# First attention: the division by the softmax sums moves from the probabilities to the outputs

## The reference, cut to what matters

```python
def dsa_mixer(x, cos, sin, w_in, w_o):       # bsz 1, L 512
    proj = x @ w_in                          # q: 16 heads x 64, k, v: 4 heads x 64, index q, k, weights
    ...
    score = jnp.einsum('bqh,bqhs->bqs', iw_b, jax.nn.relu(s))
    score = jnp.where(causal[None], score, -jnp.inf)
    _, sel = lax.top_k(score, top_k)         # top_k = 128 of up to 512 keys
    ...
    logits = jnp.einsum('bqgrd,bqkgd->bqgrk', q_b, k_sel) * A_HEAD_DIM ** -0.5
    logits = jnp.where(valid[:, :, None, None, :], logits, -jnp.inf)
    p = jax.nn.softmax(logits, axis=-1)
    o = jnp.einsum('bqgrk,bqkgd->bqgrd', p.astype(v.dtype), v_sel)
    ...
    return out @ w_o
```

## Time and profile before

| | us |
|---|---|
| median of 3 runs (1941.14 to 1942.45) | 1941.49 |
| the profiled execution | 1947.47 |
| its span | 1945.5 |
| PE busy | 1869.9 |
| DVE (VectorE) busy | 1184.5 |
| ACT (ScalarE) busy | 734.1 |
| POOL (GpSimd) busy | 136.5 |
| scores of the first unit start, in the span | 123.91 |
| output projection starts, in the span | 202.40 |

### The profile page before, as it was taken

How to read it: one execution, slowest core, us unless ns; L and a number is a source line. 1 busy time by engine, 2 the same in 40 slices (tenths; PEclk the granted TensorE clock), 3 DMA queues, 4 the chain that set the end, 5 groups by cost and what they waited for, 6 DMA issues and landing times.

```text
span 1945.5 us, 23033 instructions
## 1 busy us (share of the span) xinstructions
PE 1869.9 (96%) x9172; PEld 1507.9 (78%) x9172; DVE 1184.5 (61%) x2191; ACT 734.1 (38%) x1146; POOL 136.5 (7%) x136
## 2 busy tenths in 40 slices
PE   9989999999999999999999999789899899999997
PEld 7765788878888888788888888677556698888885
DVE  4989676555556676577544546766775554333437
ACT  4447343232223434544222223535554352222221
POOL 0343000000000151000000000000230000000000
PEclk9989999999999999999999999989999899999998
DMA  6210425434442212234343342031001413323221
GB/s 203 66 65 2 152 84 167 161 130 138 144 149 70 74 57 66 66 108 134 127 130 108 118 142 88 23 109 44 1 1 60 146 33 99 108 87 108 87 87 44
DMA packets 116874, 184.04 MB, mean 95 GB/s; under 512 B 7152, under 2 KB 71792, under 8 KB 113696
## 3 DMA queue, kind: packets, MB, share of 16 engines
q1 hardware_dynamic: 115376, 177.77, 27.7%
q0 software_dynamic: 1392, 4.82, 0.9%
HBM read 180.47 MB, written 2.10 MB: 94 GB/s over the span
## 4 chain that ended last, share of the span: by engine, by line
PE 74%; DVE 17%; ACT 5%; issue 3%; POOL 1%; DMA 0%; SPq 0%; DVEq 0%; ACTq 0%
PE bank L593 10%; PE bank L595 10%; PE bank L594 10%; PE bank L784 7%; PE bank L786 7%; PE bank L785 7%; DVE wl L1859 2%; PE bank L567 2%; PE bank L569 2%; PE bank L568 2%; DVE gb L2216 2%; DVE m L2214 1%; PE bank L843 1%; PE bank L615 1%; PE bank L617 1%
## 5 line engine op out<-in xcount | busy, mean ns | idle before, releaser
L1859 DVE TENSOR_TENSOR wl<-raw,wh 128x2048 fp32r<-128x2048 f32 (+1 forms) x138 | 310.3, 2254 | 200.6 <-ACT wh L1243 200.3
L1243 ACT ACTIVATE wh<-raw 128x2048 fp32r<-128x2048 f32 (+1 forms) x142 | 265.2, 1883 | 244.4 <-PE bank L786 90.0
L593 PE MATMUL bank<-xh,wh 128*128 128x512 f32 (+2 forms) x880 | 348.1, 396 | 2.3 <-DVE wl L1859 2.3
L594 PE MATMUL bank<-xh,wl 128*128 128x512 f32 (+2 forms) x880 | 347.0, 394 | 0.0
L595 PE MATMUL bank<-xl,wh 128*128 128x512 f32 (+2 forms) x880 | 347.0, 394 | 0.0
L786 PE MATMUL bank<-wh,ul 128*128 128x512 f32 x592 | 230.4, 389 | 0.0
L785 PE MATMUL bank<-wl,uh 128*128 128x512 f32 x592 | 230.4, 389 | 0.0
L784 PE MATMUL bank<-wh,uh 128*128 128x512 f32 x592 | 230.4, 389 | 0.0
L593 PEld LDWEIGHTS bank<-xh,wh 128*128 128x128 f32 (+2 forms) x880 | 165.3, 188 | 43.0 <-DVE wl L1859 3.1
L595 PEld LDWEIGHTS bank<-xl,wh 128*128 128x128 f32 (+2 forms) x880 | 165.2, 188 | 38.8
L594 PEld LDWEIGHTS bank<-xh,wl 128*128 128x128 f32 (+2 forms) x880 | 165.4, 188 | 38.3
(11 more groups left out here) (363 smaller groups left out, 3102.9 us busy)
## 6 DMA issues: line engine op xcount, KB each, us to landing
raw<-in_mlp_w_up SPq DMA_DIRECT2D x32, 1024.0 KB, 5.6
raw<-in_mlp_w_down SPq DMA_DIRECT2D x32, 1024.0 KB, 5.1
raw<-in_w_ada SPq DMA_DIRECT2D x24, 1024.0 KB, 5.0
raw<-in_b_w_in SPq DMA_DIRECT2D x12, 1024.0 KB, 5.4
raw<-in_w_in SPq DMA_DIRECT2D x11, 1024.0 KB, 5.2
raw<-in_w_gate SPq DMA_DIRECT2D x11, 1024.0 KB, 5.3
raw<-in_w_up SPq DMA_DIRECT2D x11, 1024.0 KB, 5.4
raw<-in_w_down SPq DMA_DIRECT2D x10, 1024.0 KB, 5.0
```

The source lines that it names most:

```text
L593: pe.matmul(o, H[:, k, c], xh[:, k, :], start=k == 0, stop=False)
L594: pe.matmul(o, L[:, k, c], xh[:, k, :], start=False, stop=False)
L1243: act.activation(slots[slot_of[i]][0][:, 0:n], raw[:, i % NRAW, 0:n], ACT.Copy).then_inc(*s_high.up(i))
L1859: dve.tensor_tensor(L[:, 0:n], raw[:, i % NRAW, 0:n], H[:, 0:n].bitcast(F), ALU.subtract).then_inc(*s_low.up(i))
```

## The change

1. The probabilities are no longer multiplied with the reciprocals of their sums. PE transposes the exponentials as they are. L2114 (VectorE) and L2761 (GpSimd) go away for this attention, and VectorE takes one reciprocal of 128 x 8 for a pair instead of eight of 128 x 1.
2. The outputs are divided instead: VectorE multiplies the bank of outputs with `inv` and writes `ob`; ScalarE and VectorE make `xh` and `xl` from `ob`. `ob` and `inv` have two buffers each, in `tmp`, where the queries of heads 8 to 15 stood until they were transposed.
3. The sums lie with queries on partitions; `inv` needs them with queries in columns on 64 partitions for each head. SP writes the 128 x 8 reciprocals of a pair to DRAM (`sums`, as single floats, 512 bytes apart in each partition), waits for that to land, and reads each head's row back into 64 partitions. This is `spread(j)`. All eight stand in the SP queue behind the fetch of chunk 12 and ahead of the fetch of chunk 13.
4. The lag is 2 instead of 3. `ob` is made 5 iterations after the last scores of a pair, `xl` 6 after them.
5. The first three iterations of the attention are written into the work ahead of it: on PE and ScalarE behind the token blocks t = 1, 2, 3 of `q` 1, on VectorE behind rounds 11, 13 and 15 of the last block. The transposes of the queries of heads 8 to 15 follow iteration 4 instead of 3.
6. GpSimd makes the low part of chunk 9, which was VectorE's. GpSimd's `rotary` uses `pl` for its temporaries instead of `gb`.

```diff
+        sums = nc.dram_tensor("sums", (8, 2, T, P), F, kind="Internal").ap()
...
-        pool_low = (5, 6, 7, 8)
+        pool_low = (5, 6, 7, 8, 9)
...
-        LAG = {"A": 3, "B": 2}
+        LAG = 2
+
+        ob, inv = [tmp[:, 0], tmp[:, 1]], [tmp[:, 2], tmp[:, 3]]
...  tensor_program
-                    w.wait_ge(*(s_pool if by_pool(key, i) else s_step).at((key, "norm", i)))
+                    if key == "A":
+                        w.wait_ge(*s_act.at((key, "exp", i)))
+                    else:
+                        w.wait_ge(*(s_pool if by_pool(i) else s_step).at((key, "norm", i)))
...
-            gemm_tok(("q", 1), 512, "x", 2)
-            drain(jobs)
+            heads = attend("A", PB1, PT1, qT, kT, lambda kb, g: vt[:, kb, g * 64:g * 64 + 64], 16, 4, True, a_ready)
+            gemm_tok(("q", 1), 512, "x", 2, after=lambda t: t and next(heads))
+            assert not jobs
+            for n, _ in enumerate(heads):
+                if n == 1:
                     turn(("qT", 1), tmp, 4, s_pool.at("rot q1"))
...  scalar_program
             def emit_a(j, ps):
-                act.activation(xh[:, j, :], ps, ACT.Copy).then_inc(*s_xhigh.up(("A", "o", j)))
+                w.wait_ge(*s_step.at(("A", "ob", j)))
+                act.activation(xh[:, j, :], ob[j % 2], ACT.Copy).then_inc(*s_xhigh.up(("A", "o", j)))
...  vector_program, attend
                     g = u - 1
+                    if key == "A":
+                        if 0 <= g < N and g % T == T - 1:
+                            j = g // T
+                            w.wait_ge(*s_act.at((key, "exp", 2 * g + 1)))
+                            dve.reciprocal(rc[:, 2 * j:2 * j + 2, :], sm[:, 2 * j:2 * j + 2, :]).then_inc(*s_step.up((key, "rc", j)))
...
+                    g = u - lag - 3
+                    if key == "A" and 0 <= g < N and g % T == T - 1:
+                        j = g // T
+                        w.wait_ge(*s_turn.at((("qT", 1), 3)))
+                        w.wait_ge(*s_mm.at((key, "o", j, 1)))
+                        w.wait_ge(s_inv, 32 * (j + 1))
+                        dve.tensor_tensor(ob[j % 2], bank[banks.of[key, "o", j]][:, :], inv[j % 2], ALU.mult).then_inc(
+                            *s_step.up((key, "ob", j)))
...  top_k
+                        if t == T - 1 and r in (11, 13, 15):
+                            next(heads)
...  gpsimd_program
+            low(9)
...
-            attend("A", PB1, 16, True)
...  sync_program
+            def spread(j):
+                w.wait_ge(*s_step.at(("A", "rc", j)))
+                sp.dma_start(sums[j].rearrange("g t q -> q g t"), att[:, 2, 2 * j:2 * j + 2, :],
+                             allow_slow_non_contiguous=True).then_inc(s_sums, 16)
+                w.wait_ge(s_sums, 16 * (j + 1))
+                if j > 1:
+                    w.wait_ge(*s_step.at(("A", "ob", j - 2)))
+                else:
+                    w.wait_ge(*s_turn.at((("qT", 1), 3)))
+                for p in range(2):
+                    sp.dma_start(inv[j % 2][64 * p:64 * p + 64, :], sums[j, p].rearrange("t q -> (t q)").partition_broadcast(64)).then_inc(s_inv, 16)
...
                 fetch(i)
+                if i == mixed[0] + 3:
+                    for j in range(8):
+                        spread(j)
```

More of the change, by code:

```diff
@@ L847, in outs @@
                         banks.drop((key, "o", j))
-                lag = LAG[key]
+                lag = LAG
                 for u in range(N + lag + 3):
@@ L1249, in turned_to, with gemm_tok @@
                     banks.read[key, j] = s_act.at((key, j))
-            def gemm_tok(key, n, evict, ticks=0, last_ticks=None, first=None):
+            def gemm_tok(key, n, evict, ticks=0, last_ticks=None, first=None, after=None):
                 k0 = 0
@@ L1263, in gemm_tok @@
                             evict(t, bank[banks.of[key, t]][:, 0:n])
+                            if after:
+                                after(t)
                         tick(jobs, ticks)
@@ L1390, in attend @@
                 nmx, sm = att[:, 0, 0:nheads, :], att[:, 1, 0:nheads, :]
-                lag = LAG[key]
-                for u in range(N + lag + 3):
+                lag = LAG
+                for u in range(N + lag + (5 if key == "A" else 3)):
                     if u < N:
@@ L1468, in scalar_program @@
             jobs.append(later(("qT", 0), 4, qT[:, 0:4, :]))
-            gemm_tok(("q", 1), 512, lambda t, ps: copy_to((("q", 1), t), tmp[:, t, :], ps), 2)
-            drain(jobs)
             def emit_a(j, ps):
-                act.activation(xh[:, j, :], ps, ACT.Copy).then_inc(*s_xhigh.up(("A", "o", j)))
-            for n, _ in enumerate(attend("A", PB1, PT1, 16, True, emit_a, ())):
-                if n == 3:
+                w.wait_ge(*s_step.at(("A", "ob", j)))
+                act.activation(xh[:, j, :], ob[j % 2], ACT.Copy).then_inc(*s_xhigh.up(("A", "o", j)))
+            heads = attend("A", PB1, PT1, 16, True, emit_a, ())
+            gemm_tok(("q", 1), 512, lambda t, ps: copy_to((("q", 1), t), tmp[:, t, :], ps), 2, after=lambda t: t and next(heads))
+            assert not jobs
+            for n, _ in enumerate(heads):
+                if n == 1:
                     turned_to(("qT", 1), 4, qT[:, 4:8, :])
@@ L2130, in attend @@
                     g = u - lag - 2
-                    if 0 <= g < N and g % T == T - 1:
+                    if key == "B" and 0 <= g < N and g % T == T - 1:
                         j = g // T
@@ L2135, in attend @@
                         banks.read[key, "o", j] = s_xlow.at((key, "o", j))
+                    g = u - lag - 3
+                    if key == "A" and 0 <= g < N and g % T == T - 1:
+                        j = g // T
+                        w.wait_ge(*s_turn.at((("qT", 1), 3)))
+                        w.wait_ge(*s_mm.at((key, "o", j, 1)))
+                        w.wait_ge(s_inv, 32 * (j + 1))
+                        dve.tensor_tensor(ob[j % 2], bank[banks.of[key, "o", j]][:, :], inv[j % 2], ALU.mult).then_inc(
+                            *s_step.up((key, "ob", j)))
+                        banks.read[key, "o", j] = s_step.at((key, "ob", j))
+                    if key == "A" and 0 <= g - 1 < N and (g - 1) % T == T - 1:
+                        j = (g - 1) // T
+                        w.wait_ge(*s_xhigh.at((key, "o", j)))
+                        emit(j)
                     yield
@@ L2225, in vector_program @@
             gemm_tok(("q", 1), None, 2)
-            drain(jobs)
-            def emit_a(j, ps):
-                dve.tensor_tensor(xl[:, j, :], ps, xh[:, j, :].bitcast(F), ALU.subtract).then_inc(*s_xlow.up(("A", "o", j)))
-            for _ in attend("A", PB1, PT1, 16, True, emit_a, [s_pool.at("rot q1")]):
+            assert not jobs
+            for _ in heads:
                 pass
@@ L2755, in attend @@
                 for i in range(nheads * T):
-                    if not by_pool(key, i):
+                    if not by_pool(i):
                         continue
```

25 lines of the change are left out of this document (15 added, 10 removed).

## The result

The changed kernel takes 1975.13 us (median of 4 runs, 1972.77 to 1978.06) against 1941.32 us (4 runs, 1940.78 to 1942.45) on the same chip: a ratio of 1.0174, 95% interval 1.0157 to 1.0192. The forecast was 1933.8 us, in a range of 1931 to 1942.5. The profiled execution took 1975.73 us and its span is 1973.9 us, 28.4 longer than the 1945.5 of before. The medians lie 33.8 us apart; the trace of before is of an execution of 1947.47 us, some 6 above its median, so 5.4 us of the 33.8 can't be placed by these two traces.

The account below looks back on a forecast made before the run. PE was taken as the bound in steady state, losing 6.69 us waiting at the start. Gains of 6.55 at the start and 1.2 in steady state, 7.75 us, took 1941.5 to 1933.8 us, range 1931 to 1942.5.

Parts of the forecast that it names:

- The trip, its store: SP's store of 1024 single floats per pair to DRAM: 3.9 to 5.9 us, within a trip taken as 7.5.
- the bound of 13.0: Upper bound in us for a pair's whole trip through DRAM, using the trace's slowest small transfer, 10.3 us.
- The reads: SP's two reads back from DRAM: 64 KB together, second issued 0.5 us later, 2.4 us.
- The rival of the slow store: VectorE's wait for `inv`: trips over 9.7 us stall pairs in turns, up to 1950.2 us; chance 0.14.
- The start: PE's 6.69 us wait before the first outputs goes; they start at about 135.0 instead of 142.42, 6.55 us won.
- The steady state: Pairs of heads in the attention: lighter VectorE lets PE run at 8.2 instead of 8.42 us, 1.2 us won.
- Behind the attention: Output projection after the last pair's trip: cost 0; over 9.8 us, each us more costs PE one, once.

Follow-up runs that it names:

- the third experiment: Changed kernel with the whole DRAM trip made, its reads landing in an unused buffer and outputs multiplied with a constant 0.01: 1958.1 us, ratio 1.0078.
- experiments four and six: Kernel before with only the interleaved start, 1945.77 us; and changed kernel with 32-byte store pieces but attention beginning only after the last projection, 1944.9 us.
- second experiment: Changed kernel with the store written as 128 pieces of 32 bytes, reads unchanged so reciprocals reach the wrong queries: 1938.12 us, ratio 0.9976.
- fifth experiment: Changed kernel with reciprocals turned into rows on VectorE and stored in 128-byte pieces by four transfers: 1937.7 us, ratio 0.9972 against the kernel before.
- the first experiment: Changed kernel without the DRAM trip, outputs multiplied with a constant 0.01 instead of the inverse sums: 1940.79 us, ratio 0.9984 against the kernel before.

## Why the prediction was wrong

**The trip, its store.** This is the step that failed: "That is 2.0 us for 64, and at twice that for a write 4.0, so the store is 3.9 to 5.9 us", and with it the bound of 13.0. Measured are 8.4 to 10.9 us for the store and 18.0 for the first trip. The price of a packet was not even too low, for the engines took 9 ns each. The working left out what comes after the engines: over 7 us until the store has landed, some 50 to 70 ns for each float that goes into one row. With the floats 64 bytes apart it is 0.9 us, with pieces of 32 bytes 0.3.

I weighed the Trainium skill's sentence that small transfers are read, modified and written as a factor of two on a packet ("DMA: Bandwidth & Descriptors", Specifications). Such rewriting of one row after another float would explain a time by the float and row; that it is the mechanism is my inference, no run shows it inside the memory. Its advice against a strided last dimension (Rules for kernel authors) agrees with the runs: contiguous pieces took 1.4 and 2.2 us, single floats 2.5 at best and 10.0 as a mean in the changed kernel.

The same page (Anatomy of one DMA, which describes transfers issued by GpSimd; these are SP's) says that a transfer's semaphore can't rise before the memory has confirmed the last byte, and puts most of a fixed 2 us down to that. That there is a part behind the packets agrees with the trace. That it is fixed does not: 1.4 us in all for the 32-byte pieces, over 7 us of silence for the single floats. I had used this page for the packets and not looked at what it says comes behind them.

**The reads.** Expected 2.4 us, for 64 KB together; each of the two brings 128 KB (64 partitions of 512 floats), which the prediction had misread. With the store in longer pieces they took 2.8 and 2.9, the second issued 0.5 later; in the changed kernel up to 8.5. The slow ones had the next store queued right behind, and none was that slow where SP waited for its reads, but one of 3.06 us had a store behind it too. What the store does to the read was not taken apart further.

**The rival of the slow store** had the mechanism right: stalls in turns, from 9.7 us on, with VectorE's product ahead of the next maxima. Its limit holds pair by pair: the trips of pairs 0, 2 and 4 were 18.0, 14.5 and 17.5 us, so 8.3, 4.8 and 7.8 over it, and PE waited 8.21, 5.47 and 7.84. Its sum was not exact: with 18.0 us for every trip it gives 33.2 + 8.2 = 41.4 us, the second term for the last pair. The trips were not all that long, and the stretch lost 35.4: 28.8 of waits, the rest not taken apart, with the slower clock behind the waits in it. That 41.4 is the medians' distance from the forecast (41.3 us) is luck. Nor does it have the queue: SP starts a pair's store only when the one before has landed and its reads are issued, 11.7 us a pair in the third experiment. It had 0.14 because its price was bounded from a row for loads. Its own argument for it, many engines writing into the same 512-byte rows as "the one thing without a row", was the right one, and should have carried more weight than an average of loads.

**The start.** Right: first outputs 135.30 against about 135.0, PE's pieces of idle 0.4 to 0.5 us, clock 1.00. The mask took 0.42 us where I took 1.0. And the two halves of the change need each other here, as experiments four and six show in the orders that were run.

**The steady state.** The 1.2 us were not there. With no wait on the trip, pairs take 8.47 us (second and fifth experiment), against 8.42 as a mean before. "PE's own work is 8.2 us for a pair" was read from one interval of 8.29, 155.93 to 164.22; the next ones are 8.53 and 8.29, and they alternate:

```profile
172.75 0.70 PE L818 MATMUL bank<-A 64*128 64x256 f32 x4
...
181.04 0.70 PE L818 MATMUL bank<-A 64*128 64x256 f32 x4
```

And PE waits 0.9 us for ScalarE's copy ahead of the last outputs in every run with the moved division, with the trip and without it, where before it waited at most 0.3 us in the attention's last pair; the prediction has no term for this. From the first experiment:

```profile
195.72 0.40 PE L854 MATMUL bank<-A 128*64 128x256 f32 x1 [0.92 <-ACT A L1359]
```

So the gain without the slow store is 202.40 - 195.75 = 6.65 us at the output projection (fifth experiment) where the sum had 7.75, and in medians 1942.71 - 1937.7 = 5.0, in the second experiment 3.2. Why the medians keep less than the trace is left open; what differs is the clock granted hundreds of us behind the change. In the stretch from 1500 to 1600 us it was 0.95 in the trace of the second experiment, which from the output projection on took 1739.2 us, and 0.91 in those of the fifth and of before, which took 1743.3 and 1743.1.

**Behind the attention.** "Cost: 0" was conditional on a trip under 9.8 us. The 6.57 us ahead of the last outputs are not this term: they are the stall of pair 6, whose `inv` lets VectorE go on at 225.41, and 0.9 us of them are there without the trip too. The last pair's trip was 223.13 to 238.07, 14.9 us, so 5.1 over the 9.8. PE lost only 0.65 of them, at chunk 10. One reason is that its last outputs had themselves been held up by pair 6: the last store was issued 7.5 us before they ended (230.68), not 4:

```profile
225.41 0.69 DVE L2166 TENSOR_TENSOR A<-bank,A 128x512 f32<-128x512 f32 x1 [5.56 <-DMA A<-sums]
...
238.17 0.69 DVE L2166 TENSOR_TENSOR A<-bank,A 128x512 f32<-128x512 f32 x1 [10.69 <-DMA A<-sums]
```

```profile
243.78 0.50 PE L728 MATMUL bank<-wh,xh 128*128 128x512 f32 x1 [0.65 <-DVE wl L1878]
```

## What to carry to other kernels

A DMA is not over when its engines are. For a small store look in the trace whether the time from issue to landing is filled with packets; if not, no rate of packets bounds it, and here the addresses set the price. When single values of many partitions must go to DRAM, turn them into rows first (0.21 us on VectorE here) or store them as they lie, and don't let many partitions write neighbouring floats of one row (10.0 us here, as a mean). Ask of a queue that waits for its own transfers how long it takes for each pair, and not only how long one trip may be. And read the steady state over several periods before taking a difference to the shortest one as idle time.

## What the hardware showed beyond that

- 1024 single floats to DRAM took 8.4 to 10.9 us, of which the 16 DMA engines moved packets in some 0.6; the same 4 KB took 1.4 us in pieces of 32 bytes and 2.2 in pieces of 128 bytes through four transfers.
- Some 50 to 70 ns for each float that goes to one row of 512 bytes (a stretch of 1 or 2 KB would fit too), alike with four rows and with eight.
- A queue that waits for its own small stores delays what is behind them far away: 17.52 us of PE's time, up to 248.18, for trips that SP had left by 226.
